# Panel order in the gates' stage, and where the second layer's context is loaded, transposed and modulated

## The reference, cut to what matters

```python
def first_block(x, c, ctx, ...):
    mod_x = silu(c) @ ada_w + ada_b                     # 6 rows of 1024
    hc, hx = modulate(rms_norm(ctx), ...), modulate(rms_norm(x), ...)
    o_x = gdn_scan(hx @ w_in[:, qkv...], state of gdn_scan(hc ...))
    z, u, v, gates = split(hx @ w_in[:, COL_Z:])        # 1024, 1024, 1024, 2048 columns
    y_gdn = rms_norm(o_x, gdn_norm_g) * silu(z)
    y_sgu = gelu(u) * (sgu_w @ layer_norm(gelu(v)) + sgu_b)
    x = x + mod_x[2] * (sigmoid(g_a) * (y_gdn @ w_a) + sigmoid(g_b) * (y_sgu @ w_b)) @ w_o
    x = x + mod_x[5] * hier_moe(modulate(rms_norm(x), mod_x[3], mod_x[4]), ...)
    return rms_norm(x, final_norm_g)

def second_block(x, c_2, ctx_2, ...):                   # xc = ctx_2
    mod = silu(c_2) @ w_ada[l] + b_ada[l]; mod_c = silu(c_ctx_2) @ w_ada[l] + b_ada[l]
    # layer 0
    q, k, v, g_a, xb, b_g, c_g, g_b = split(modulate_2(x, shift, scale) @ w_in)
    hc = modulate_2(xc, shift_c, scale_c)               # h * (1 + scale) + shift
    ... = split(hc @ w_in)
    # attention, short convolution, w_out, layer norm; layer 1 is a gated recurrence
```

## Time and profile before

| | |
|---|---|
| device time, median of 3 runs | 1771.29 us (1769.92 to 1771.68) |
| the profiled execution, device time | 1775.53 us |
| its span, first to last instruction | 1773.8 us |
| PE busy | 1546.5 us (87%) |
| VectorE busy | 812.2 us (46%) |
| ScalarE busy | 371.3 us (21%) |
| gates' stage | about 469 to 615 us of the span |
| merge stage | about 616 to 731 us |
| end of the experts, final norm, mod0 | about 1047 to 1077 us |

### The profile page before, as it was taken

One profiled execution on the slowest core, in us unless ns is written; L12 is line 12 of the kernel. 1 busy time (PEld: TensorE's weight loads), 2 busy tenths in 40 slices (PEclk: granted clock), 3 DMA queues, 4 the chain that ended last, 5 costly groups with the idle time before them and its releaser, 6 DMA issues. The chain is left out here.

```text
span 1773.8 us, 19527 instructions
## 1 busy us (share of the span) xinstructions
PE 1546.5 (87%) x7573; PEld 901.5 (51%) x7573; DVE 812.2 (46%) x1512; ACT 371.3 (21%) x700; POOL 190.3 (11%) x280
## 2 busy tenths in 40 slices
PE   4999968789999698876789868999889899999977
PEld 2877756578644344442234323444444447656563
DVE  2344548444536558632111123356564315576553
ACT  3222245111111100110000011000450124642230
POOL 0000016500000000001000000000350001212340
PEclk9899989677899799787899988999999899999998
DMA  9331002230577677579999992524311222121120
GB/s 351 98 95 48 1 1 50 84 85 11 183 260 258 235 275 246 226 309 411 408 366 367 388 344 103 190 95 159 103 37 35 95 68 75 48 95 48 49 72 24
DMA packets 132299, 283.62 MB, mean 160 GB/s; under 512 B 28744, under 2 KB 39272, under 8 KB 126955
## 3 DMA queue, kind: packets, MB, share of 16 engines
q1 hardware_dynamic: 128608, 266.65, 42.1%
q0 software_dynamic: 3600, 15.73, 2.2%
HBM read 312.77 MB, written 4.19 MB: 179 GB/s over the span
## 5 line engine op out<-in xcount | busy, mean ns | idle before, releaser
L2707 PE MATMUL ps<-hT,ring 128*128 128x512 f32 x256 | 114.8, 606 | 3.1 <-PEq L2614 2.7
L1395 PE MATMUL ps<-ring,hTx 128*128 128x512 f32 x256 | 112.1, 594 | 1.9 <-PEq L176 1.8
L327 DVE SCALAR_TENSOR_TENSOR ada_acc<-ring,cact,ada_acc 128x512 f32<-128x512 f32 x154 | 104.1, 747 | 0.5
L631 PE MATMUL ps<-hTx,ring 128*128 128x256 f32 x384 | 91.6, 394 | 5.3 <-PEq L176 5.3
L2342 PE MATMUL ps<-hT,ring 128*128 128x512 f32 x208 | 90.4, 592 | 0.0
L631 PEld LDWEIGHTS ps<-hTx,ring 128*128 128x128 f32 x384 | 75.1, 198 | 19.8 <-issue 8.0
L2707 PEld LDWEIGHTS ps<-hT,ring 128*128 128x128 f32 x256 | 48.9, 194 | 62.9 <-issue 62.9
L1395 PEld LDWEIGHTS ps<-ring,hTx 128*128 128x128 f32 x256 | 48.3, 191 | 60.5 <-issue 60.5
L1928 PE MATMUL ps<-ring,hTx 128*32 128x512 f32 x384 | 53.8, 711 | 26.0 <-DMA ring<-in_expert_w 26.0
L722 DVE SCALAR_TENSOR_TENSOR conv<-xpad,taps,conv 128x512 f32<-128x512 f32 (+1 forms) x96 | 63.6, 663 | 3.4
L2342 PEld LDWEIGHTS ps<-hT,ring 128*128 128x128 f32 x208 | 39.5, 190 | 48.5 <-issue 48.3
(11 more groups left out here) (528 smaller groups left out, 2745.8 us busy)
## 6 DMA issues: line engine op xcount, KB each, us to landing
ring<-in_expert_w SPq DMA_DIRECT2D x24, 2048.0 KB, 15.4
far<-in_expert_w SPq DMA_DIRECT2D x24, 2048.0 KB, 18.2
ring<-in_w_in SPq DMA_DIRECT2D x16, 2048.0 KB, 11.6
ring<-in_ada_w SPq DMA_DIRECT2D x12, 2048.0 KB, 9.5
ring<-in_w_ada SPq DMA_DIRECT2D x12, 2048.0 KB, 9.3
ring<-in_w_in_c SPq DMA_DIRECT2D x10, 2048.0 KB, 7.9
ring<-in_expert_w POOLq DMA_DIRECT2D x32, 512.0 KB
far<-in_expert_w POOLq DMA_DIRECT2D x32, 512.0 KB
```

What stands on the lines that cost most here:

```text
L327: ins = dve.scalar_tensor_tensor(out=part, in0=slot[:, kt], scalar=c[:, kt:kt + 1], in1=part, op0=ALU.mult, op1=ALU.add)
L631: ins = pe.matmul(ps[:, j % BANKS, s * L:(s + 1) * L], slot[:, kt, (j % 4) * P:(j % 4 + 1) * P], (hTc, hTx)[s][:, kt], start=(kt == 0), st ...
L1395: ins = pe.matmul(ps[:, 2 + i % BANKS], hTx[:, kt, t * P:(t + 1) * P], stream.slot(n)[:, kt], start=(kt == 0), stop=(kt == KT - 1))
L2707: ins = pe.matmul(bank, slot[:, kt, j % 4 * P:(j % 4 + 1) * P], hT[:, kt], **edge)
```

## The change

**The panels of the gates' stage** are added as U0, R0, U1, R1, and so on to U7, R7. The recurrence's two views of lent slots (`slot_a`, `slot_b`) and the order in which they are freed are exchanged with it, so that the slot that comes free first is again the one that U1 (now the third panel, not the second) goes to; a new method `issue_ahead` issues U1 from the scan's block ahead of R0. On PE each total comes one panel earlier: total(0) after U1, total(6) after U7, and total(7) alone behind it. DVE's order of work is what it was.

**The context** (`ctx_2`, 1 MB) is loaded by SP in the experts' block, behind the two panels issued after `half_up`, into a tile of its own on the right side of SBUF. The second panel of `w_in_ab` (three DMAs) and the wait for `d_done` before it go from there to the final norm's block, behind the load of `grow`. In the final norm's block PE transposes `cs` into banks 4 to 7, and ACT modulates all eight parts behind its square root. `mod0` does only x. `hT` is allocated from the start, and `hTx` and `otok` are its two halves. `mod1` does both sequences, as before.

**The taps** of the layer-0 block: PE transposes them after the first panel's projections instead of before, and DVE copies them after dot(0) and then waits for the biases, where it did both before dot(0).

```diff
 Stream
+    def issue_ahead(self, sp, n):
+        sp.wait_ge(self.used[n % RING], n // RING)
+        self.load(sp, n)
+        self.ahead.add(n)
...
-        for i in range(9):
-            if i < 8:
-                uvg.append(len(stream.panels))
-                add_cols(w_in, COL_Z + (2 + i) * PANEL)
-            if i:
-                rest.append(len(stream.panels))
-                add_cols(ada, (3 + i) * PANEL)
+        for i in range(8):
+            uvg.append(len(stream.panels))
+            add_cols(w_in, COL_Z + (2 + i) * PANEL)
+            rest.append(len(stream.panels))
+            add_cols(ada, (4 + i) * PANEL)
...
+        hT = sb(whole, "hT", [P, KT, 2 * L])
-            hTx = sb(first, "hTx", [P, KT, L])
-            otok = sb(first, "otok", [P, TT, D])
+            hTx = hT[:, 0:KT // 2].rearrange("p k t -> p (k t)").rearrange("p (k t) -> p k t", k=KT)
+            otok = hT[:, KT // 2:].rearrange("p k t -> p (k t)").rearrange("p (t d) -> p t d", t=TT)
...
-                                    stream.issue(sp, uvg[1] + 1)
+                                    stream.issue_ahead(sp, uvg[1])
...
-                                if i // TT >= 2:
-                                    total(pe, i // TT - 2)
+                                if i // TT:
+                                    total(pe, i // TT - 1)
...
-                        total(pe, 6)
                         total(pe, 7)
...
 experts' block, SP
-                            sp.wait_ge(d_done, 2 * N)
-                            stream.issue(sp, ab_in[0] + 3)
+                            sp.dma_start(cs[:, :, :], w["ctx_2"][0].rearrange("(t p) d -> p t d", p=P)).then_inc(ctx_in, 16)
...
 final norm's block
                             sp.dma_start(grow[:, :], row_bcast(w["final_norm_g"])).then_inc(loaded, 16)
+                            stream.issue(sp, ab_in[0] + 3)
+                        @block.tensor
+                        def _(pe):
+                            pe.wait_ge(ctx_in, 16)
+                            for b in range(4):
+                                transpose_in(pe, 4 + b, lambda i: cs[...], 4).then_inc(turned_c, 1)
...
                             act.activation(stat[:, 2:4], stat[:, 2:4], ACT.Sqrt).then_inc(std, 1)
+                            for kt in range(KT):
+                                if kt % 2 == 0:
+                                    act.wait_ge(turned_c, kt // 2 + 1)
+                                act.activation(hT[:, kt, 0:L], ps[:, 4 + kt // 2, ...], ACT.Identity, scale=..., bias=...)
...
-            modulate_block("mod0", 0, True)
+            modulate_block("mod0", 0, (0,))
...
 layer 0, PE
-                            pe.wait_ge(taps_loaded, 16)
-                            for j in range(AT):
-                                ins = pe.transpose(ps[:, 6, 3 * j:3 * j + 3], taps_row[...], ident[0:3, 0:3])
-                            ins.then_inc(turned, 1)
...
                                         if last_panel == 0:
+                                            pe.wait_ge(taps_loaded, 16)
+                                            for m in range(AT):
+                                                ins = pe.transpose(ps[:, 6, 3 * m:3 * m + 3], taps_row[...], ident[0:3, 0:3])
+                                            ins.then_inc(turned, 1)
                                             pe.wait_ge(taps_done, 1)
...
 layer 0, DVE
+                            dot(dve, 0)
                             dve.wait_ge(turned, 1)
                             dve.tensor_copy(taps[...], ps[:, 6, ...]).then_inc(taps_done, 1)
                             dve.wait_ge(bias_loaded, 32)
-                            dot(dve, 0)
```

43 lines of the change are left out of this document (21 added, 22 removed).

## The result

The changed kernel takes 1745.09 us (median of 3 runs, 1743.31 to 1746.19) against 1771.29: a ratio of 0.9853, with an interval of 0.983 to 0.9875. The forecast was 1749.9. The profiled execution took 1746.19 us, with a span of 1744.5 (before: 1775.53 and 1773.8).

What follows compares the result with a forecast made beforehand. PE, busy 87% of the span, was taken to bound the kernel; 15.2 us from the panels (part A) plus 6.2 from context and taps (part B) gave 21.4, taking 1771.29 to 1749.9, range 1745 to 1761.

Steps and rivals of the forecast that it cites:

- those transposes: Gates' stage: PE's transposes of `otok` run at the high clock, 1.91 us instead of 3.68, gaining 1.8.
- The end: Gates' stage end: dot(7) is done before PE's last matmul, so total(7) takes total(6)'s place, gaining 6.7 us.
- U2 late: Gates' stage: panel U2, issued after dot(0), lands after PE is ready, costing 0.6 us, between 0 and 2.6.
- Merge start: Merge stage's first matmuls start with a warmer PE clock, gaining 2.0 us, between 0 and 3.3.
- Norm earlier: Final norm: DVE starts sooner after PE's last experts' product, with one DMA issue left there, gaining 2.7 us.
- ACT's eight modulations: Final norm: ACT modulates all eight context parts behind its square root and ends after DVE, costing 1.4 us.
- The clock term of -0.8: Layer 0's start: PE's first matmuls follow one burst of transposes, not two, costing 0.8 us, between 0 and 3.3.
- U waits for DVE: Rival, gates' stage: DVE delays dots, slots free late, PE waits at U3 to U7, some 8 us; 1758, 10%.
- it needs 14.0 us of the 15.1: Gates' stage: a U panel's load takes 14.0 us of PE's 15.1 on the panel before, leaving 1 us spare.
- Part B gives nothing: Rival, final norm: context and taps edits gain nothing because SP stays last or `grow` or context comes late; 1756, 10%.
- Slower, the pair shared evenly: Rival, gates' stage: paired loads share DMA engines evenly, U3 to U7 each 3.8 us late, costing 28.0; 1777.9, 3%.
- Not doing what it says: Rival, gates' stage: another wait holds `gated` or dot(7), so only the context and taps gain remains; 1765, 2%.

Runs made afterwards that it cites:

- e4: The kernel before, unchanged, run and traced once more; 1764.11 us in a single run.
- e5: The changed kernel with two unused DVE multiplications after each of the eight `rest` dots, before its slot is given back; 1747.86 us, ratio 0.9869.
- e2: The kernel before with only the context and taps edits, keeping the old panel order and totals; 1761.60 us, ratio 0.9941.

## Why the prediction was right, step by step

**Part A.** *Wait before the mix, wait before `otok`, those transposes*: 0.6, 4.9 and 1.8 predicted, 0.60, 4.92 and 1.77 found. *The end*: 6.7 and total(7) at the high clock 1.0, together 7.7; from the first total behind the last panel to the merge stage it was 615.75 - 603.22 = 12.53 and is 600.85 - 596.01 = 4.84, so 7.69. *U2 late*: 0.6 predicted, 1.23 found, within its bounds. I gave the load 9.2 us from 489.8; SP issued it at 488.23 and it landed at 497.95, 9.7 later. In us behind the stage's start PE is ready at 29.3 and the panel there at 30.5. The stage without the merge's start was to gain 13.2 and gained 13.35.

*Merge start*: 2.0 taken between 0 and 3.3, as it was open whether the clock would hold; found 2.93. It held at that start in all eight profiled executions that have part A and the biases in one piece, and had fallen in the three with the old order and nothing added (31.00 to 31.02). The second clock term of the stage, 3.0 at `w_out`, was not in the sum at all: the wait of 3 us there is no part of the change, only the moment of it. In `e4` and `e5` those 16 records took 8.7 to 8.8, so that 3.0 is its size against one of two traces of the kernel before and 1.6 against the other.

**Part B.** *Norm earlier*: 2.7, found 4.50 - 0.79 = 3.7, because I took the barrier at 1.83 from another stage and DVE passes it sooner. *ACT's eight modulations*: -1.4, found 3.74 us of ACT and 0.9 on the path; the cover in time held, as the context was turned by 1038.75 at the latest and ACT never waited. *mod0 without the context, no wait for the taps' DMA, clock*: 4.9 + 1.5 - 0.8 = 5.6 and the taps -0.7. From the start of x's transposes to layer 0 it was 12.11 and is 5.35, 6.8 gained with 0.5 paid behind the first panel. The clock term of -0.8 was wrong: layer 0's first 128 records take 29.36 us, as the 29.38 before. The norm gained 9.5 where the terms in it gave 7.7; against `e4`, where the context's transposes were warm (1.97 us, not 3.67), it gained 8.0.

**What was missing** is the change of the later stages: "a stage elsewhere gave the time back" stood only in the last sentence, as something that would prove me wrong. It happened in part and did not decide. So did another of its signs of being wrong, PE's wait for `in_w_in` at U2, which the sum itself had priced. Layer 0, the residual, mod1 and the end gave back 4.6 us between `before` and `after`, of which the sum had 1.5. Against these 3.1 stand 0.9 and 3.0 more in the merge and 1.8 more in the norm: 21.4 becomes 24.0. The two series have 26.2 and 25.0, and what is left between is less than the stages ahead of the gates', the routing and the experts differ between two executions of one kernel (up to 3.4, 3.8 and 2.1 us). Against `e4` in place of `before` the same stages give 13.2 + 4.0 + 8.0 less 0.8, 1.7, 0.7 and 1.2, which is 20.8. So the forecast was right by its mechanism, but that it came as close as it did is in part luck: 3.1 us of loss and 5.7 of gain stood outside the sum, and which trace of the kernel before one takes moves the account from 24.0 to 20.8.

**The rivals.** *U waits for DVE*: refuted. No panel behind U2 is late, and `e5` shows that even 2.35 us more on each dot makes none late. The spare of 1 us was not even all the same: in the changed kernel U4 lands 2.1 us before PE asks for it and U6 0.4. The step "it needs 14.0 us of the 15.1" was wrong in kind: 14.0 was measured with R's transfer ahead of U's, and counting it again from a later issue counts R twice. *Part B gives nothing*: refuted by `e2`, 10.4 us. *Slower, the pair shared evenly*: refuted for the changed kernel, where the R panels land in 10.1 us at the median and no U behind U2 comes late. Its price of 5 x 5.6 counted every U as late anew, where a delay of one U is also cover for the next two; `e5` was made to test that and had no second wait at all, so the price stays untested. *Not doing what it says*: refuted by the rows above.

## What to carry to other kernels

When two loads stand behind each other in a queue, count from the first one's issue: here the second was issued 1.1 and 3.2 us late at no cost, while the first one's 8.8 us were running. Move the last consumers of a long sum up by one step so that the stage does not end on a chain of two engines, and look for the dearer half of such a wait in the clock of what follows it. And price every later start of a stage at both clocks: in this kernel, with its many gaps of 1 to 3 us, traces with a shift of 0.7 to 4 us had other starts cold, and that was worth up to 6 us, as much as a real edit.
